# The merge stage's gate product by seven half-size products with summed operands, and the branch product in four pieces after it

## The reference

```
h = modulate(rmsnorm(h_res, pre_mix_g[l]), sh1, sc1)
proj = h @ w_in[l]
q_r, k_r, v_r, g_r, q_s, k_s, v_s, a_r, a_s = jnp.split(proj, split_pts, axis=-1)
...
mixed = (jax.nn.sigmoid(a_r) * (ret @ w_ret_branch[l])
         + jax.nn.sigmoid(a_s) * (sb @ w_sb_branch[l]))
y = mixed @ w_out[l]
```

## Time and profile before

| | |
|---|---|
| median of 3 runs | 1691.95 us |
| the profiled execution's own time | 1691.52 us |
| its span | 1689.7 us |
| TensorE busy | 1650.5 us (98%) |
| VectorE, ScalarE, GpSimd busy | 1054.0, 662.4, 752.9 us |
| mean granted clock | 0.997 |
| merge stage, TensorE's first matmul to the first of the output projection | 749.92 to 930.86 us |

### The profile page before, as it was taken

How to read it: one execution, slowest core, us unless ns; L and a number is a source line. 1 busy time by engine, 2 the same in 40 slices (tenths; PEclk the granted TensorE clock), 3 DMA queues, 4 the chain that set the end, 5 groups by cost and what they waited for, 6 DMA issues and landing times.

```text
span 1689.7 us, 25207 instructions
## 1 busy us (share of the span) xinstructions
PE 1650.5 (98%) x9680; PEld 1370.3 (81%) x9680; DVE 1054.0 (62%) x1350; ACT 662.4 (39%) x1130; POOL 752.9 (45%) x311
## 2 busy tenths in 40 slices
...
GB/s 353 26 56 95 39 79 60 88 311 212 270 219 205 99 228 41 163 38 137 50 50 50 164 186 143 236 120 269 230 310 198 261 243 205 301 158 349 91 293 100
DMA packets 62133, 284.12 MB, mean 168 GB/s; under 512 B 7892, under 2 KB 8788, under 8 KB 51928
## 3 DMA queue, kind: packets, MB, share of 16 engines
...
...
## 4 chain that ended last, share of the span: by engine, by line
PE 76%; DVE 11%; DMA 4%; issue 3%; ACT 3%; POOL 1%; SPq 1%; ACTq 0%; POOLq 0%; DVEq 0%
PE ps L885 6%; PE ps L887 6%; PE ps L886 6%; PE ps L1294 6%; PE ps L1296 6%; PE ps L1295 6%; PE ps L971 5%; PE ps L1339 4%; PE ps L1338 4%; PE ps L1337 4%; PE ps L972 4%; PE ps L973 4%; DMA ada_r<-ada_rows 2%; PE ps L1175 2%; DVE acc L2133 2%
## 5 line engine op out<-in xcount | busy, mean ns | idle before, releaser
L1294 PE MATMUL ps<-w_hi,f_hi 128*128 128x512 f32 x440 | 174.8, 397 | 4.6 <-issue 2.7
L1296 PE MATMUL ps<-w_hi,f_lo 128*128 128x512 f32 x440 | 174.4, 396 | 0.0
L1295 PE MATMUL ps<-w_lo,f_hi 128*128 128x512 f32 x440 | 174.4, 396 | 0.0
L650 POOL TENSOR_TENSOR w_hi<-raw,zero 128x1024 fp32r<-128x1024 f32 x34 | 68.7, 2019 | 230.6 <-PE ps L887 112.9
L663 POOL TENSOR_TENSOR w_lo<-raw,w_hi 128x1024 fp32r<-128x1024 f32 x16 | 41.7, 2615 | 229.7 <-ACT w_hi L1417 202.5
L738 POOL TENSOR_TENSOR w_lo<-w,w_hi 128x1024 fp32r<-128x1024 f32 x34 | 85.0, 2505 | 110.1 <-ACT w_hi L1826 65.0
L1339 PE MATMUL ps<-ring,w_hi 128*128 128x512 f32 x336 | 134.0, 399 | 0.0
L1338 PE MATMUL ps<-ring,w_lo 128*128 128x512 f32 x336 | 132.4, 394 | 0.0
L1337 PE MATMUL ps<-ring,w_hi 128*128 128x512 f32 x336 | 131.7, 392 | 0.0
L2092 DVE TENSOR_TENSOR_SCAN uu<-uu 128x512 f32<-128x512 f32 (+7 forms) x96 | 99.9, 1082 | 37.7 <-ACT uu L1510 37.6
L2517 DVE TENSOR_TENSOR hid<-hid,ps 128x512 f32<-128x512 f32 x48 | 32.7, 683 | 131.2 <-PE ps L1339 131.2
...
## 6 DMA issues: line engine op xcount, KB each, us to landing
...
raw<-wstream SPq DMA_DIRECT2D x104, 512.0 KB, 3.5
ada_r<-ada_rows SPq DMA_DIRECT2D x32, 512.0 KB, 4.9
w<-wstream SPq DMA_DIRECT2D x32, 512.0 KB, 3.3
extra<-aops SPq DMA_DIRECT2D x12, 1024.0 KB, 7.7
r_lo<-aops SPq DMA_DIRECT2D x10, 1024.0 KB, 6.1
r_hi<-aops SPq DMA_DIRECT2D x10, 1024.0 KB, 8.4
aops<-as_r ACTq DMA_DIRECT2D x16, 512.0 KB, 3.7
```

The lines of the kernel that those rows point to most:

```text
L1294: nc.tensor.matmul(bank, fh, wh, start=start, stop=False, skip_group_check=skip)
L1295: nc.tensor.matmul(bank, fh, wl, start=False, stop=False, skip_group_check=skip)
L1296: return nc.tensor.matmul(bank, fl, wh, start=False, stop=stop, skip_group_check=skip)
```

## The change

The gate product, formerly 4 pieces of 4 tiles over 8 chunks, is now done first as a whole, as seven products (`A_P1`, `A_P2`, `A_P6`, `A_P7`, `A_P5`, `A_P4`, `A_P3`, called P1, P2 and so on below, in this order). Each has 4 tiles m over 4 chunks, 48 matmuls. P1 and P2 take blocks V11 and V21 of the weights and blocks of h; P4 a block of h; P6, P7, P5 and P3 sums of h from `aops`, loaded into `extra` and into the place of a block of h in a_hi and a_lo that is no longer needed (`a_sums`). P6, P7, P5 and P4 need sums of weight blocks: VectorE makes them in place (`a_step`), 2, 1, 1 and 3 steps, each step on two halves h, with the value in `w_val` and the other term in `raw[h]`. The products alternate between slots 2, 3 and 0, 1 of the weights (`a_slot`). GpSimd makes both parts of P1 and P2; for the others ScalarE makes the high part (`a_high`) and GpSimd the low one.

P6 and P7 add to P1's banks, P3 to P5's; ScalarE copies intermediate results out (`a_copy`), VectorE adds the rest (`a_add`), ScalarE applies the sigmoid in SBUF (`a_sigmoid`). The branch follows in four pieces in the order of `MERGE_ORDER`. `MIX` and the waits at the output projection follow that order.

```diff
-MERGE_G, MERGE_TILES = 4, 8
+MERGE_G, MERGE_TILES = 4, 4
+MERGE_ORDER = (2, 3, 0, 1)
...
-MIX = [(c, slice(0, S)) for c in range(6)] + [(c, slice(th * HALF, (th + 1) * HALF)) for th in range(2) for c in (6, 7)]
+MIX = [(c, slice(0, S)) for c in (4, 5, 6, 7, 0, 1)] + [(c, slice(th * HALF, (th + 1) * HALF)) for th in range(2) for c in (2, 3)]
...
+A_P1, A_P2, A_P6, A_P7, A_P5, A_P4, A_P3 = range(7)
+V11, V12, V21, V22 = range(4)
+A_VALUE = (V11, V21, V12, V22, V12, V22, V22)
+A_STEPS = {A_P6: ((V11, "-"), (V22, "from")), A_P7: ((V12, "-"),), A_P5: ((V11, "-"),), A_P4: ((V12, "-"), (V11, "+"), (V21, "-"))}
+A_STEP_AT = {A_P6: 0, A_P7: 4, A_P5: 6, A_P4: 8}
+A_SUMMED = {A_P6: 3, A_P7: 5, A_P5: 7, A_P4: 13}
+A_RAW, A_SUM, A_PHI, A_WHI, A_WLO = (2 * RET_G, 5 * RET_G), 4 * RET_G, 2 * RET_G, 7 * RET_G, 9 * RET_G
+A_X, A_Z = (6, 7, 0, 1), (2, 3, 4, 5)
+A_BANKS = (A_X, A_Z, A_X, A_X, A_Z, A_X, A_Z)
+A_QUAD = ((0, 0), (1, 1), (0, 1), (1, 0))
...
+        def a_slot(n, h):
+            return 2 * ((n + 1) % 2) + h
+        def gated(c, th):
+            return (al_f if c < 4 else ah_f)[:, c % 4, th * HALF:(th + 1) * HALF]
...
+            def a_value(n, *after):
+                sp.wait_ge(*after)
+                if n in (A_P2, A_P6):
+                    sp.wait_ge(r_wph, A_PHI + 2 * n)
+                elif n > A_P6:
+                    sp.wait_ge(r_wsum, A_SUM + A_STEP_AT[n - 1] + 2)
+                for h in range(2):
+                    sp.dma_start(w_val[:, a_slot(n, h), :], wstream[2 * (PC_AR + A_VALUE[n]) + h, :, :]).then_inc(ar_val[h], 16)
+            def a_raw(n, step):
+                last = A_STEP_AT[n] + 2 * step - 2
+                for h in range(2):
+                    if last >= 0:
+                        sp.wait_ge(r_wsum, A_SUM + last + h + 1)
+                    sp.dma_start(raw[:, h, :], wstream[2 * (PC_AR + A_STEPS[n][step][0]) + h, :, :]).then_inc(ret_raw[h], 16)
+            def a_sums(o, slot, *after):
+                sp.wait_ge(*after)
+                for part, a in enumerate((a_hi, a_lo)):
+                    dst = extra[:, part, :, :] if slot == 0 else a[:, 4:8, 0:HALF]
+                    sp.dma_start(dst.bitcast(f32), aops[o, :, part, :, :]).then_inc(rr_in[slot], 16)
             sp.wait_ge(r_wlo, 9 * RET_G)
+            a_value(A_P1, gemm_done, TL_MERGE - 4)
+            a_raw(A_P6, 0)
+            a_sums(0, 0, gemm_done, TL_MERGE - 4)
+            a_value(A_P2, gemm_done, TL_MERGE)
+            a_value(A_P6, ar_mm, 4)
+            a_raw(A_P6, 1)
+            a_raw(A_P7, 0)
+            a_value(A_P7, ar_mm, 8)
+            a_sums(1, 1, ar_mm, 8)
+            a_raw(A_P5, 0)
+            a_value(A_P5, ar_mm, 12)
+            a_sums(2, 0, ar_mm, 12)
+            a_raw(A_P4, 0)
+            a_value(A_P4, ar_mm, 16)
+            a_raw(A_P4, 1)
+            a_raw(A_P4, 2)
+            a_sums(3, 1, ar_mm, 16)
+            a_value(A_P3, ar_mm, 20)
+            sp.wait_ge(r_wsum, A_SUM + 14)
...
-            piece(PC_MERGE, RAW_MERGE // 2 + 1, 0, TL_MERGE - 4)
-            piece(PC_MERGE + 1, RAW_MERGE // 2 + 2, 1, TL_MERGE)
-            with pool.Fori(1, MERGE_G) as g:
-                for j, slot, free in ((0, 0, -4), (1, 1, 0)):
-                    piece(PC_MERGE + 2 * g + j, RAW_MERGE // 2 + 2 * g + j + 1, slot,
-                          TL_MERGE + MERGE_TILES * g + free)
+            def a_low(n, h):
+                slot = a_slot(n, h)
+                nc.gpsimd.tensor_tensor(w_lo4[:, slot, :], w_val[:, slot, :], w_hi4[:, slot, :].bitcast(f32), ALU.subtract).then_inc(r_wlo, 1)
+            for n in (A_P1, A_P2):
+                for h in range(2):
+                    pool.wait_ge(ar_val[h], 16 * (n + 1))
+                    nc.gpsimd.tensor_tensor(w_hi4[:, a_slot(n, h), :], w_val[:, a_slot(n, h), :], zero[:, 0:1].broadcast_to([P, RAW]), ALU.add).then_inc(r_wph, 1)
+                    pool.wait_ge(r_wph, A_PHI + 2 * n + h + 1)
+                    a_low(n, h)
+            for n in (A_P6, A_P7, A_P5, A_P4, A_P3):
+                for h in range(2):
+                    pool.wait_ge(r_whi, A_WHI + 2 * (n - A_P6) + h + 1)
+                    a_low(n, h)
+            for i in range(MERGE_G):
+                if i < 2:
+                    pool.wait_ge(ar_mm, 24 + 4 * i)
+                piece(PC_MERGE + i, RAW_MERGE // 2 + i + 1, i % 2, None if i < 2 else TL_MERGE + MERGE_TILES * (i - 1))
...
-            def last_r(j):
-                for u in ((0, 1), (2,), (3,), ())[j]:
-                    r_transposed(RET_G - 1, u)
-            piece_T(PC_MERGE, 0, a_hi, a_lo, lambda j: None if j < 2 else (ev_dve, EV_MERGE - 5 + j), bank=gate_bank, after=last_r)
+            def a_operand(n, k):
+                if n in (A_P6, A_P5):
+                    return tuple(extra[:, part, k, :] for part in range(2))
+                c, th = {A_P1: (0, 0), A_P4: (4, 1)}.get(n, (4, 0))
+                return tuple(a[:, c + k, th * HALF:(th + 1) * HALF] for a in (a_hi, a_lo))
+            def a_free(n, m):
+                if n == A_P1:
+                    return None if m < 2 else (ev_dve, EV_MERGE - 5 + m)
+                if n == A_P2:
+                    return (ev_dve, EV_MERGE - 1 + m) if m < 2 else (r_gated, 4 * RET_G - 3 + m)
+                return {A_P6: (ar_copy, m + 1), A_P7: (ar_copy, 4 + m + 1), A_P5: (ar_add, m + 1), A_P4: (ar_copy, 8 + m + 1), A_P3: (ar_add, 4 + m + 1)}[n]
+            for n in range(7):
+                start = n in (A_P1, A_P2, A_P5, A_P4)
+                if n in (A_P6, A_P7):
+                    pe.wait_ge(rr_in[n - A_P6], 32 * 7)
+                if n in (A_P5, A_P3):
+                    pe.wait_ge(rr_in[0 if n == A_P5 else 1], 32 * 8)
+                for m in range(4):
+                    h, out_ = m // 2, ps[:, A_BANKS[n][m], :]
+                    if m % 2 == 0:
+                        pe.wait_ge(r_wlo, A_WLO + 2 * n + h + 1)
+                    if a_free(n, m) is not None:
+                        pe.wait_ge(*a_free(n, m))
+                    for k in range(4):
+                        wh, wl = (w[:, a_slot(n, h), k * 256 + m % 2 * P:k * 256 + (m % 2 + 1) * P] for w in (w_hi4, w_lo4))
+                        last = passes(out_, wh, wl, *a_operand(n, k), start and k == 0, k == 3, not start)
+                    last.then_inc(ar_mm, 1)
+                    for u in {(A_P1, 0): (0, 1), (A_P1, 2): (2,), (A_P1, 3): (3,)}.get((n, m), ()):
+                        r_transposed(RET_G - 1, u)
             pe.wait_ge(r_lo_done, 4 * RET_G)
...
+            for i in range(MERGE_G):
+                piece_T(PC_MERGE + i, i % 2, r_hi, r_lo,
+                        lambda j: (ar_add, 8 + 4 * i + j + 1) if i < 2 else (ev_dve, EV_MERGE + 4 * (i - 2) + j + 1),
+                        bank=lambda j: ps[:, (A_X, A_Z)[i % 2][j], :])
...
+            def a_high(n, h):
+                act.wait_ge(*((ar_val[h], 16 * (n + 1)) if n == A_P3 else (r_wsum, A_SUM + A_SUMMED[n] + h)))
+                nc.scalar.activation(w_hi4[:, a_slot(n, h), :], w_val[:, a_slot(n, h), :], ACT.Copy).then_inc(r_whi, 1)
+            def a_copy(n, c, th):
+                for m in range(4):
+                    act.wait_ge(ar_mm, 4 if n == A_P1 else 4 * n + m + 1)
+                    nc.scalar.activation(gated(c + m, th), ps[:, A_X[m], :], ACT.Copy).then_inc(ar_copy, 1)
+            def a_sigmoid(q):
+                fh, th = A_QUAD[q]
+                for m in range(4):
+                    act.wait_ge(ar_add, 4 * q + m + 1)
+                    nc.scalar.activation(gated(4 * fh + m, th), gated(4 * fh + m, th), ACT.Sigmoid).then_inc(ar_sig, 1)
+            a_copy(A_P1, 0, 0)
+            a_high(A_P6, 0)
+            a_high(A_P6, 1)
+            a_high(A_P7, 0)
+            a_high(A_P7, 1)
+            a_copy(A_P6, 4, 0)
+            a_sigmoid(0)
+            a_high(A_P5, 0)
+            a_high(A_P5, 1)
+            a_copy(A_P7, 0, 1)
             act.wait_ge(r_lo_done, 4 * RET_G)
             act.dma_start(m1[:, :, :], m1_dram[:, :, :]).then_inc(m1_in, 16)
...
+            for n in (A_P4, A_P3):
+                for h in range(2):
+                    a_high(n, h)
+            for q in range(1, 4):
+                a_sigmoid(q)
             for u, (c, cols) in enumerate(MIX):
-                act.wait_ge(gl_mm, 2 + (12 if u < 6 else 14 if u < 8 else 16))
+                act.wait_ge(gl_mm, 2 + (4 * (u // 2 + 1) if u < 6 else 14 if u < 8 else 16))
                 nc.scalar.activation(a_hi[:, c, cols], m1[:, c, cols], ACT.Copy).then_inc(mix_hi, 1)
...
-            def merge(g, after=None):
+            def a_step(n, step):
+                src, how = A_STEPS[n][step]
+                done = A_STEP_AT[n] + 2 * step
+                turn = sum(len(A_STEPS[q]) for q in A_STEPS if q < n) + step
+                for h in range(2):
+                    value = w_val[:, a_slot(n, h), :]
+                    dve.wait_ge(ret_raw[h], 16 * (A_RAW[h] + turn + 1))
+                    if step == 0:
```

(61 more changed lines are left out.)

37 lines of the change are left out of this document (14 added, 23 removed).

## The result

The changed kernel takes 1701.92 us (median of 6 runs, 1698.48 to 1705.25) against 1692.26 (6 runs, 1690.72 to 1695.28) of the kernel before: a ratio of 1.0055, 95% interval 1.0041 to 1.0070. It is slower by 0.55%, and above the predicted range, whose upper end was 1700. The profiled execution took 1702.22 us, 10.70 above that of before.

The account below looks back on a forecast made before the run. TensorE, busy 98% of the span, was taken as the bound, the stage lasting as long as its matmuls. -11.2 - 0.75 + 1.3 + 0 + 11.1 + 2.6 = +3.05 on 1691.52 gave 1694.6, median 1695.0, range 1688.5 to 1700.

Parts of the forecast that it names:

- Removed, -11.2: Gate product: seven products of 48 matmuls take 78.4 us where four pieces took 89.6, saving 11.2 us.
- P4, three steps, +11.1: Ahead of P4: its weight-sum chain takes 22.3 us, both terms' loads slowed by `m1`; TensorE waits 11.1 us.
- the rival on the other side: Ahead of P4: `m1` does not slow the loads, wait 6.3 us, total 1687.6, up to 1690.2 with clock loss; chance 0.20.
- P6, +1.3: Ahead of P6: gating and two sum steps end 12.5 us after P2 began; TensorE waits 1.3 us (0.5 to 2.5).
- The clock, +2.6: At P4's start: TensorE's clock falls to half rate around the long wait, costing 2.6 us, three quarters of 3.4.
- For the short wait before P6 I count nothing: At P6: no loss of clock was counted for the short wait ahead of it, 0 us.
- No wait at P7, P5, P3 and the branch: Ahead of these products and the branch's pieces: weights arrive in time, 0 us; P5 at most 0.5.
- the rival of a second late chain: At P3 and the branch's first piece: P3's value lands 5 us later, P3 waits 1.5; total 1696.5 to 1700; chance 0.20.
- the 0.02 for slower products: Seven products: they miss the pieces' pace, or some unseen cover makes the whole neutral; chance 0.02.
- The end of the stage, -0.75: Output projection's first tile: its wait vanishes because six of ten parts are split two tiles or more earlier, saving 0.75 us.

Follow-up runs that it names:

- e3: As e1, but P6's and P4's weight sums have one step each (V22, V11, V21 left out; other result, same matmuls): 1679.56 us, 0.9929 of the kernel before.
- e1: The changed kernel with ScalarE's 4 MB load of `m1` issued after P3's high parts: 1692.38 us, 1.0013 of the kernel before.
- e2: The changed kernel with the `m1` load in its place but split into eight DMAs of one chunk each: 1698.66 us, 1.0049 of the kernel before.
- e8: The changed kernel with VectorE's second-half V22 sum for P6 waiting for GpSimd's first-half low part: 1702.50 us, 1.0062 of the kernel before.
- e6: The changed kernel with P6's V22 loaded early into part of `m1`'s place, its two sums back to back: 1698.46 us, 1.0043 of the kernel before.

## Why the prediction was wrong, step by step

The sum said 1694.6 for the profiled execution; it took 1702.22. The 7.6 between them, by the prediction's own steps:

- **Removed, -11.2:** right. The products run at the pace wherever nothing is waited for, and e3 gives the stage without the chains: 170.64.
- **P4, three steps, +11.1: this is the step that failed, +4.3.** Its structure held: the chain value, term, term, high part, low part, with each load behind the sum before it, is what TensorE waits for. The loads were sized wrongly. I wrote that "both terms" fall into the load of `m1` and gave 3.3 to the value. The value is issued in the same instant as `m1` and took 11.8 us to its sum; the terms took 4.2 and 3.2, where the earlier trace rows had 5.7 for one issued beside the large load. Against the sum of 22.3 us: +8.5 on the value, -1.6 and -2.6 on the terms, 26.6. (The sum has 0.1 from each sum to the next issue, so a term is compared with 5.8.) I had the time of `m1`'s issue, 0.7 us after P7's end, and did not put it beside the value's, 0.1 us after; in the trace both came 0.2 after. And the 5.7 came from a load issued at 778.98, 8.1 us behind `m1`, when some 3 of its 4 MB were moved, as the rival on the other side noted itself. e1 shows the cause, e2 how the value lost its bandwidth. Without these 4.3 us the median of 1701.92 would be 1697.6, inside the range.
- **P6, +1.3:** measured 2.5, at the upper end of its bounds of 0.5 to 2.5. Of the missing 1.2, 0.9 is the low part that stood behind the second half's sum: e8 removes it and finds 1.5. The other 0.3 is VectorE's gating, whose end came 3.3 us after P2's start (763.40, first sum at 766.73) where I had put 3.0.
- **The clock, +2.6:** at P4 right in kind and near in size, 2.1; the three quarters were a guess, and over the five kernels with a long wait there (e1, e2, the changed one, e6, e8) P4 lost 1.6 to 2.5. "For the short wait before P6 I count nothing" was wrong: 1.6. Both together make 3.7.
- **No wait at P7, P5, P3 and the branch:** right: in the changed kernel TensorE waits ahead of none of them (P7 and P3 take 11.20 each, and what P6 and P4 have above that is clock). So the rival of a second late chain came nearest in size (1696.5 to 1700) for a reason that did not occur, which is luck. (Its piece of the branch takes by the earlier trace rows up to 2 x (1.97 + 2.73) = 9.4 us, not 9; nothing hung on it. And the 0.02 for slower products is counted under "faster", where it doesn't belong.)
- **The other side, loads not slowed by `m1`:** refuted here. Its P4 wait of 6.3 is what e1 measured with `m1` out of the way (6.05).
- **The end of the stage, -0.75:** the projection's first tile runs without a wait, as said, but the rest after the stage is only 0.26 shorter. It holds the 3.4 us at 0.50 from 1180.3, worth some 1.6 (an estimate from the same loss in P6), and over the ten kernels it is 757.8 to 758.9, so what the term is worth can't be told.

Together: 4.3 for P4's loads, 1.2 for P6's wait, 1.6 - 0.5 for the clock, 0.5 for the end, and 0.6 for the stage's start make 7.7, the 7.6 but for rounding.

The passage of the Trainium skill that I weighed ("TensorE: Matmul & The Clock Gate", HAM oscillation) describes longer waits, 3 to 5 us in its example. For the wait ahead of P4 the trace agrees: TensorE resumed at 0.50. The rows go further: the clock also fell at the waits of 2.0 to 2.8 us ahead of P6 (e8: of P7), and not at every wait of that length (last section).
